# The large parts of four weight chunks, laid 4112 bytes apart instead of 4096

## What is computed

```
h    = rmsnorm(x, g_pre_mix)
proj = h @ w_in                                  # 2048 x 12824
y_a  = nsa_attention(...)                        # 8 heads: compressed, selected, window
y_b  = retention(...) * silu(rg)                 # 4 heads
y_c  = memory_attention(mq, mem_n @ w_mem_kv)    # 4 heads, 256 memory tokens
merged = bgate0 * (y_a @ w_br_nsa) + bgate1 * (y_b @ w_br_ret) + bgate2 * (y_c @ w_br_mem)
x  = x + rmsnorm(merged @ w_o, g_post_mix)
u  = causal_dwconv(rmsnorm(x, g_pre_ffn) @ w_up) # width 3, 2 x 5632 channels
x  = x + rmsnorm((gelu(u_gate) * u_val) @ w_down, g_post_ffn)
```

## Time and profile before

| | |
|---|---|
| median of three runs | 1696.08 us |
| profiled execution | 1696.61 us, of which the span of instructions 1694.8 us |
| TensorE busy | 1685.0 us (99%), 8842 matmuls |
| TensorE loading weights | 1453.6 us (86%) |
| VectorE busy | 1128.4 us (67%) |
| ScalarE busy | 830.7 us (49%) |
| GpSimd busy | 49.6 us (3%) |
| DMA | 327.95 MB, mean 194 GB/s |
| TensorE's granted clock | 0.999 of full over the span |

### The profile page before, as it was taken

The page is one execution under the profiler, slowest core; times in us unless marked ns, Lnnn a source line. Parts: engine busy times, 40 slices in busy tenths (PEclk is TensorE's granted clock), DMA queues, the critical chain, the costliest instruction groups (busy, mean ns, idle before and its releaser), DMA issues.

```text
span 1694.8 us, 24997 instructions
## 1 busy us (share of the span) xinstructions
PE 1685.0 (99%) x8842; PEld 1453.6 (86%) x8842; DVE 1128.4 (67%) x1534; ACT 830.7 (49%) x1139; POOL 49.6 (3%) x55
## 2 busy tenths in 40 slices
PE   9999999999999999999999999999999999999998
PEld 8888899998888888888888888888888888888886
DVE  7755576767575544554565787677776786776777
ACT  7544455544434444444444665555455455554453
POOL 1000000000140000000000000000000000000000
PEclk9999999999999999999999999999999999999999
DMA  9576478445656667666557556565565665665564
GB/s 293 183 246 203 133 237 262 117 147 174 211 162 185 195 192 210 201 195 190 185 188 245 180 188 198 181 199 195 187 202 171 190 210 186 190 195 176 189 199 148
DMA packets 241917, 327.95 MB, mean 194 GB/s; under 512 B 12907, under 2 KB 159116, under 8 KB 241292
## 3 DMA queue, kind: packets, MB, share of 16 engines
q1 hardware_dynamic: 241804, 326.47, 62.0%
HBM read 321.71 MB, written 3.67 MB: 192 GB/s over the span
## 4 chain that ended last, share of the span: by engine, by line
PE 94%; DMA 2%; DVE 2%; ACT 1%; issue 1%; POOL 0%; POOLq 0%; DVEq 0%; ACTq 0%
PE bank L1532 22%; PE bank L1523 16%; PE bank L1521 16%; PE bank L1522 16%; PE bank L1541 12%; PE bank L1552 2%; DMA wraw<-in_cmp_w_v 1%; PE bank L1557 1%; PE bank L1496 1%; PE bank L1495 1%; PE bank L1497 1%; DVE wlo L930 1%; DMA wraw<-in_cmp_w_k 1%; ACT whi L614 1%; PE bank L1721 0%
## 5 line engine op out<-in xcount | busy, mean ns | idle before, releaser
L930 DVE TENSOR_TENSOR wlo<-wraw,whi 128x1024 fp32r<-128x1024 f32 x584 | 708.0, 1232 | 450.3 <-ACT whi L614 291.2
L614 ACT ACTIVATE whi<-wraw 128x1024 fp32r<-128x1024 f32 x584 | 614.1, 1058 | 548.5 <-PE bank L1523 389.7
L1532 PE MATMUL bank<-hx,whi 128*128 128x512 f32 x1504 | 350.7, 390 | 0.0
L1532 PEld LDWEIGHTS bank<-hx,whi 128*128 128x128 f32 x1504 | 280.0, 188 | 57.0 <-DVEq L1053 0.2
L1521 PE MATMUL bank<-whi,hx 128*128 128x512 f32 x512 | 201.6, 394 | 0.0
L1523 PE MATMUL bank<-whi,hx 128*128 128x512 f32 x512 | 199.4, 389 | 0.0
L1522 PE MATMUL bank<-wlo,hx 128*128 128x512 f32 x512 | 199.2, 389 | 0.0
L1541 PEld LDWEIGHTS bank<-hx,wlo 128*128 128x128 f32 x1504 | 186.9, 192 | 3.7
L1541 PE MATMUL bank<-hx,wlo 128*128 128x256 f32 x1504 | 188.7, 283 | 0.0
L1521 PE MATMUL bank<-whi,r_hi 128*128 128x512 f32 x384 | 149.8, 390 | 0.0
L1522 PE MATMUL bank<-wlo,r_hi 128*128 128x512 f32 x384 | 149.5, 389 | 0.0
(11 more groups left out here) (275 smaller groups left out, 1799.8 us busy)
## 6 DMA issues: line engine op xcount, KB each, us to landing
wraw<-in_w_in SPq DMA_DIRECT2D x200, 512.0 KB, 4.0
wraw<-in_w_up SPq DMA_DIRECT2D x176, 512.0 KB, 4.5
wraw<-in_w_down SPq DMA_DIRECT2D x88, 512.0 KB, 4.7
wraw<-in_w_mem_kv SPq DMA_DIRECT2D x32, 512.0 KB, 4.8
wraw<-in_w_o SPq DMA_DIRECT2D x32, 512.0 KB, 4.3
wraw<-in_w_br_mem SPq DMA_DIRECT2D x16, 512.0 KB, 4.3
wraw<-in_w_br_nsa SPq DMA_DIRECT2D x16, 512.0 KB, 4.3
wraw<-in_w_br_ret SPq DMA_DIRECT2D x16, 512.0 KB, 4.4
```

What stands on the lines that cost most here:

```text
L614: nc.scalar.activation(whi[:, c], wraw[:, c], ACT.Copy).then_inc(hi_done, 1)
L930: V.tensor_tensor(wlo[:, c], wraw[:, c], whi[:, c].bitcast(F32), ALU.subtract).then_inc(lo_done, 1)
L1532: e = T.matmul(ps[pair[u]][:, :], whi[:, c, k, u * P:(u + 1) * P], x2[:, :, 4 * c + k, :], start=c == 0 and k == 0, stop=False, skip_group ...
```

## The change

`whi` was a tensor of four chunks of 1024 elements. It becomes a tensor `high` of 4352 elements (the name in SBUF stays `whi`), and `whi` a view of it: chunk c starts at element 1028 c, 4112 c bytes, and has 1024 elements as before. The four elements between two chunks aren't used, nor are those behind the last.

```diff
@@ constants
 EPS = 1e-6
+HIGH_PITCH = CK * GW + 4
@@ def build
         wraw = sb("wraw", [P, 4, CK, GW])
-        whi, wlo = (sb(n, [P, 4, CK, GW], F32R) for n in ("whi", "wlo"))
+        high = sb("whi", [P, 4 * CK * GW + 256], F32R)
+        whi = high[:, 0:4 * HIGH_PITCH].rearrange("p (c n) -> p c n", c=4)[:, :, 0:CK * GW].rearrange("p c (k n) -> p c k n", k=CK)
+        wlo = sb("wlo", [P, 4, CK, GW], F32R)
         arena = sb("arena", [P, 12288])
```

## The result

The changed kernel takes 1713.47 us (median of 4 runs, 1713.31 to 1713.73), the kernel before 1695.99 us beside it: the ratio is 1.0103, with a 95% interval of 1.0085 to 1.0120. It is 17.5 us slower. Forecast was 1696.1 us and a range that ended at 1700.3.

What follows compares the result with a forecast made beforehand. TensorE, at work 99% of the span, was taken to bound the kernel. Moving 0, weights 0 and VectorE and ScalarE 0 left the median of 1696.1 us unchanged, with a range of 1694.3 to 1700.3 us.

Steps and rivals of the forecast that it cites:

- What bounds the kernel: Whole kernel: TensorE at work 99% of the span, so only matmul distance or late weight chunks could change the time.
- TensorE, moving: 0, bounds 0 to +6.0 us: TensorE streaming whi, 2016 matmuls from chunks 1 to 3: shifted starts cost 0, at most 3 ns each, 6.0 us.
- TensorE, weights: 0, bounds -1.6 to +0.2 us: TensorE loading whi as weights, 1608 loads from shifted chunks: no cost, between -1 and +1 ns each.
- Nothing is tied to the present place of whi that could be given back: Streamed whi, wlo and hx: equal lengths of 389 to 390 ns, so the moving term could not fall below 0.
- The first rival: TensorE pays for each shifted stream by fetching another 64-byte block: 1702.1 or 1709.6 us, chance 10%.
- VectorE and ScalarE: 0: VectorE's subtraction reading whi and ScalarE's copy writing it: off the path while TensorE is full, 0 (-0.1 to 0) us.
- the second rival: The common 4096-byte pitch of wraw, whi and wlo was costing something; leaving it gains 3.6 us, 1692.5 us, chance 3%.
- The Trainium skill's 16-byte lines: Cited SBUF rule penalizing each crossing to a new 16-byte line; shifts of 16, 32 and 48 bytes would cost 0.

Runs made afterwards that it cites:

- e3: TensorE-only kernel, streamed and held operands shifted separately or together; with 512 columns 226.7 ns per matmul unshifted, 233.3 ns with either one 32 bytes off.
- e9: Third TensorE-only kernel: wide-product stream patterns, equal shifts, other widths; streams at 32, 0, 32 bytes on unshifted tiles average 232.2 ns, against 226.7 ns unshifted.
- e2: Changed kernel with whi's chunks 4160 bytes apart, all on multiples of 64: 1719.84 us, 1.0141 of the kernel before.
- e4: Kernel before with 32 bytes of padding ahead of hx, so hx and all behind it lie 32 bytes further on: 1695.93 us, ratio 1.0000.
- e5: Second TensorE-only kernel, offsets from -32 to +512 bytes and mixed patterns: 226.7 ns at 256 bytes apart, 231.7 and 233.5 ns with both operands alternating.
- e11: TensorE-only kernel, 512 columns, alternating by 32 bytes: stream alone 229.9 ns, weights alone 235.0 ns, both together every 2nd matmul 231.6 ns.

## Why the prediction was wrong

*What bounds the kernel* held. TensorE is full before and after, only the distance between matmuls moved, and no wait took part.

*TensorE, moving: 0, bounds 0 to +6.0 us* is the step that failed first. Measured: +11.9 us, over 3576 wide matmuls. The streams of whi alone have +7.1, already above my bound, and a third of these matmuls stream wlo, +4.7, and weren't in my count at all. I priced the shift from L1887 and L1891, plain fp32 with 256 columns. By e3 and e9 the loss is one of 448 columns and more in fp32r; narrower streams don't show it or gain. The rows were the nearest ones by address and the wrong ones by width. I had named the type as a reason to keep the upper end and not the width. What plain fp32 does at 512 columns wasn't tried, so the part of the type is open. The range had a slip of its own: 1696.1 less 1.6 is 1694.5 and plus 4.0 is 1700.1, where it says 1694.3 and 1700.3; it changes nothing here.

*TensorE, weights: 0, bounds -1.6 to +0.2 us*: measured +6.2 us (L1535 and L1555). The same mistake: the gate columns (L1736, L1737) have 256 columns and bound nothing for 512. Their -2 and -1 ns against L1495 and L1496 were differences of printed lengths; from start to start the mean is 119.8 ns, against 119.9 in L1495 to L1497, so to take 0 from them was a fair reading of that width. By e3 a held operand always 32 bytes off under 256 columns is 118.4 ns and not 120. The argument that a load of 188 ns is covered by 226.7 ns was no argument either: in e3 a shift of the weights alone by 32 bytes makes 226.7 into 233.3 ns.

*"Nothing is tied to the present place of whi that could be given back"* was right as far as the runs go, and I drew half of the conclusion. (The page also has 394 ns for L1521 over hx, which the prediction's "389 to 390" leaves out; from start to start, without its long gaps, it has the same 226.8 to 227.2.) All of hx, mx, r_hi, r_lo, whi and wlo lie 128 bytes past a multiple of 256, and their tiles step by multiples of 512 bytes. Equal lengths over all of these pairs didn't say that places don't matter; all pairs had the same place, so the trace held no pair from which it could be read. The one exception among the fp32r operands was wg, whose tiles step by 192 bytes, and its rows show it if single distances are read and not means. The timeline of the kernel before:

```profile
45.13 0.28 PE L1737 MATMUL bank<-hx,wg 128*128 128x256 f32 x1
45.25 0.29 PE L1736 MATMUL bank<-hx,wg 128*128 128x256 f32 x1
45.38 0.28 PE L1737 MATMUL bank<-hx,wg 128*128 128x256 f32 x1
```

The starts are 120 and 130 ns apart here and 113 to 127 over the whole loop, with the mean of 119.8, where the matmuls of the earlier trace rows have 120 again and again. In the changed kernel L1544, whose operands share their place, goes 117, 118, 121, 120, 124 with the same mean of 120 behind the shifted pass.

*The first rival* had the sign and the place (TensorE, streams, chunks 1 to 3, ScalarE and VectorE unchanged), with 10%, and at its two prices 1702.1 and 1709.6 us. Its mechanism, one more block of 64 bytes, is wrong: e2 has no operand off such a block and is slower still, e4 has all of them off and loses nothing. And it foresaw 226.7 ns in chunk 0, which has up to 228.5 in the streams of whi. That it had the sign was luck.

*VectorE and ScalarE: 0* was right, with 1233 and 1060 ns. So was the part of the second rival that was argued against it: the common place modulo 4096 cost nothing, and leaving it gave nothing back.

*The Trainium skill's 16-byte lines* ("SBUF — State Buffer", SBUF cachelines) gave 0 for shifts by whole lines. The traces don't agree: 32, 64 and 128 bytes are whole lines and cost 2.2 to 6.7 ns per matmul depending on which operand is moved, and the period that they show is 256 bytes. What agrees is that a stream 4 bytes off is the slowest, 236.9 ns; one 8 bytes off has 233.3, no more than one 32 bytes off. By that rule the sum would be 1696 us; measured is 1713.

What stays open is the mechanism. Shown are the place (TensorE alone), the period of 256 bytes, that both operands enter, that streams of up to 384 columns don't lose where it was tried, and that aligned matmuls behind a shifted stretch can be off their 226.7 ns for ten distances and more. That two readers of one memory get into each other's way would fit; it wasn't shown, and e5 and e11 didn't tell which of the accesses meet.

## What to carry to other kernels

Where TensorE is full and matmuls are fp32r with 512 columns, put streamed and held operands at the same place modulo 256 bytes, and both on a multiple of 32: tensor starts, pitches and offsets of slices. Padding by an odd amount, which looks free, costs 1 to 4.5% per matmul here, and a multiple of 64 is no safe choice. For other widths time it: 448 and 480 columns behaved otherwise. Before a term is set to 0 by a like row, ask in which respects the row is like: a row with another width and another type bounds nothing, and if all rows agree because all share one property, they say nothing about changing it.

## What the runs showed of the hardware

- Aligned fp32r matmuls stand at their columns plus 32 cycles of 2.4 GHz: 146.7, 173.3, 220.0 and 226.7 ns for 320, 384, 496 and 512 columns, and 120.0 for 256 (e3, e9).
- With 512 columns most other distances of the operands modulo 256 bytes cost 2.2 to 7.6 ns, and a stream 4 bytes off 10.2 ns; a held operand 16 bytes up or down costs nothing. Equal shifts of both are free by 32, 64, 96, 128 and 192 bytes and cost 3.4 to 6.2 ns by 8, 16 and 48 (e3, e5, e9).
- The matmuls at a common place that follow a shifted stretch are 224 to 241 ns apart for a while, from no distance at all to ten and more, depending on the shift (e3, e5, e9).
- With 256 columns operands apart are faster than operands together, 117.1 to 118.7 against 120.0 ns (e3, e5, e9).
- A width of 448 or 480 has 202.7 and 216.6 ns at a common place, more than columns plus 32 cycles (200.0 and 213.3).
- VectorE's and ScalarE's durations didn't change for shifts by 16, 32, 48, 64 or 128 bytes (1232 to 1234 and 1058 to 1061 ns).
